# The router of a mixture of experts reads the raw residual instead of the normed one

## The reference

```python
x = x + concatenate([y_d, y_m]) @ w_out
h = rms_norm(x, norm2_g)            # x * rsqrt(mean(x*x) + 1e-6) * norm2_g
g_logits = h @ router_group         # [256, 4], softmax, argmax: the token's group
e_logits = h @ router_expert[g]     # 8 logits of that group, the 2 largest win
# each token goes to 2 of 32 experts; expert: (silu(h @ w_gate) * (h @ w_up)) @ w_down
x = x + weighted sum of the two experts' outputs
```

## Time and profile before

| What | us |
|---|---|
| median of 3 runs | 1144.38 |
| lowest and highest | 1142.68, 1144.67 |
| the profiled execution | 1147.17 |
| its span, first to last instruction | 1145.4 |
| busy in the span: PE, DVE, ACT, POOL | 1077.5, 568.5, 413.7, 48.3 |
| mean granted clock of TensorE | 0.97 of full |

### The profile page before, as it was taken

One profiled execution on the slowest core, in us unless ns is written; L12 is line 12 of the kernel. 1 busy time (PEld: TensorE's weight loads), 2 busy tenths in 40 slices (PEclk: granted clock), 3 DMA queues, 4 the chain that ended last, 5 costly groups with the idle time before them and its releaser, 6 DMA issues.

```text
span 1145.4 us, 13701 instructions
## 1 busy us (share of the span) xinstructions
PE 1077.5 (94%) x5547; PEld 819.3 (72%) x5547; DVE 568.5 (50%) x712; ACT 413.7 (36%) x518; POOL 48.3 (4%) x56
## 2 busy tenths in 40 slices
PE   7996889999999999999999999958899999999996
PEld 6885875544444457888887998837688887888885
DVE  5667552222222236444445448387665654454453
ACT  4446231111111133343343445363344334334332
POOL 2430000000000000000000000010100000000000
PEclk9998999999999999999999999867899999999999
DMA  8961087989999937655655455411075545555540
GB/s 285 300 230 74 15 352 314 366 350 404 415 414 408 421 118 243 188 179 183 187 179 183 135 182 172 150 42 38 1 236 186 184 147 161 188 182 181 186 147 37
DMA packets 101814, 239.51 MB, mean 209 GB/s; under 512 B 11666, under 2 KB 56810, under 8 KB 86282
## 3 DMA queue, kind: packets, MB, share of 16 engines
q1 hardware_dynamic: 99850, 229.05, 55.5%
q0 software_dynamic: 1920, 9.85, 2.5%
HBM read 237.81 MB, written 3.43 MB: 211 GB/s over the span
## 4 chain that ended last, share of the span: by engine, by line
PE 87%; DVE 8%; ACT 3%; issue 1%; POOL 1%; POOLq 0%; DVEq 0%; ACTq 0%
PE banks L924 20%; PE banks L926 19%; PE banks L925 19%; PE banks L1127 10%; PE banks L1142 5%; PE banks L1108 3%; PE banks L1117 3%; PE banks L931 2%; PE banks L1242 1%; PE banks L1056 1%; DVE token_major L1457 1%; PE banks L943 1%; PE banks L1025 1%; PE banks L1009 1%; DVE head_stats L1603 1%
## 5 line engine op out<-in xcount | busy, mean ns | idle before, releaser
L1477 DVE TENSOR_TENSOR weights_lo<-raw_weights,weights_hi 128x2048 fp32r<-128x2048 f32 x116 | 265.7, 2292 | 229.1 <-ACT weights_hi L616 228.9
L616 ACT ACTIVATE weights_hi<-raw_weights 128x2048 fp32r<-128x2048 f32 x116 | 221.6, 1912 | 194.6 <-PE banks L926 184.6
L924 PE MATMUL banks<-weights_hi,normed_T_hi 128*128 128x512 f32 (+1 forms) x624 | 247.2, 396 | 5.0 <-DVE stage L1793 3.1
L926 PE MATMUL banks<-weights_hi,normed_T_lo 128*128 128x512 f32 (+1 forms) x624 | 242.8, 389 | 0.0
L925 PE MATMUL banks<-weights_lo,normed_T_hi 128*128 128x512 f32 (+1 forms) x624 | 242.3, 388 | 0.0
L924 PEld LDWEIGHTS banks<-weights_hi,normed_T_hi 128*128 128x128 f32 x624 | 118.1, 189 | 36.6 <-issue 10.1
L926 PEld LDWEIGHTS banks<-weights_hi,normed_T_lo 128*128 128x128 f32 x624 | 117.8, 189 | 24.8
L925 PEld LDWEIGHTS banks<-weights_lo,normed_T_hi 128*128 128x128 f32 x624 | 117.9, 189 | 22.5
L1127 PE MATMUL banks<-expert_weights,stage 128*64 128x512 f32 x256 | 113.2, 595 | 0.0
L924 PE MATMUL banks<-weights_hi,ffn_hidden_T_hi 128*128 128x512 f32 x176 | 68.6, 390 | 3.0 <-DVE ffn_hidden_T_lo L1797 3.0
L925 PE MATMUL banks<-weights_lo,ffn_hidden_T_hi 128*128 128x512 f32 x176 | 68.5, 389 | 0.0
(11 more groups left out here) (306 smaller groups left out, 1573.6 us busy)
## 6 DMA issues: line engine op xcount, KB each, us to landing
raw_weights<-in_w_in SPq DMA_DIRECT2D x38, 1024.0 KB, 5.2
raw_weights<-in_ffn_w_gate SPq DMA_DIRECT2D x44, 512.0 KB, 3.9
raw_weights<-in_ffn_w_up SPq DMA_DIRECT2D x44, 512.0 KB, 4.9
raw_weights<-in_ffn_w_down SPq DMA_DIRECT2D x22, 1024.0 KB, 4.8
expert_weights<-in_w_gate SPq DMA_DIRECT2D x16, 1024.0 KB, 7.3
expert_weights<-in_w_up SPq DMA_DIRECT2D x16, 1024.0 KB, 9.5
expert_weights<-in_w_down SPq DMA_DIRECT2D x16, 1024.0 KB, 9.6
stage<-in_w_down SPq DMA_DIRECT2D x9, 1024.0 KB, 11.5
```

Of the source, the lines that this page charges most:

```text
L616: ins = eng.activation(w_hi[:, slot, :], raw, ACT.Copy)
L924: eng.matmul(dst, x[0], w[0], start=first_one, stop=False)
L926: return eng.matmul(dst, x[1], w[0], start=False, stop=last_one)
L1477: ins = eng.tensor_tensor(w_lo[:, slot, :], raw, w_hi[:, slot, :], ALU.subtract)
```

## The change

The router reads `res` itself, and what the norm does to it is put elsewhere. The weight of the norm, `norm2_g`, is loaded a second time as one number per feature (`route_gain`) and multiplied into the router's weights on DVE; rstd is applied to the logits when DVE takes them from PSUM. So PE can transpose `res` as soon as it is complete. The ten warming matmuls ahead of the transposes are gone. ACT squares a tile and splits a tile in turn. The normed rows `tok` are now made after the low parts of `routed_T`, and their own low part is made by POOL instead of DVE.

```diff
+        route_gain = sb("route_gain", [P, KT])
 @@ SP, after the pieces 3 to 5
+            eng.dma_start(route_gain[:, :], A["norm2_g"][0].rearrange("(p k) -> p k", k=KT)).then_inc(router_loaded, 16)
 @@ POOL
             eng.wait_ge(normed, TILES * (N2 + 1))
             load_gain("ffn1_norm_2")
+            for t in range(TILES):
+                eng.wait_ge(tok_hi, t + 1)
+                eng.tensor_tensor(tok_parts[1][:, t], tok[:, t, :].rearrange("p (d k) -> p k d", k=KT), tok_parts[0][:, t],
+                                  ALU.subtract).then_inc(tok_lo, 1)
 @@ ACT, c == 3 of the projection loop
-                    eng.wait_ge(router_loaded, 16 * (1 + GROUPS))
+                    eng.wait_ge(router_gained, 1)
 @@ ACT, behind w_out
-            square(N2, lambda t: (gemm_used, 3 + t))
-            t8_split(T_N2, routed_T)
+            square_of(0)
+            raw_split(0)
+            square_of(1)
+            raw_split(1)
             for t in range(TILES):
+                eng.wait_ge(normed, TILES * N2 + t + 1)
                 eng.activation(tok_parts[0][:, t], tok[:, t, :].rearrange("p (d k) -> p k d", k=KT), ACT.Copy).then_inc(tok_hi, 1)
 @@ PE
             eng.wait_ge(gemm_used, 3)
-            stay_warm(10, 0)
-            transpose8(T_N2, tok, lambda t: (normed, TILES * N2 + t + 1), True)
+            transpose8(T_N2, res, lambda t: (gemm_used, 3 + t), True)
             stay_warm(8, 2)
 @@ DVE, projection loop
+                if c == 2:
+                    eng.wait_ge(router_loaded, 16 * (2 + GROUPS))
+                    eng.tensor_tensor(router[:, :, :], router[:, :, :], wide(route_gain[:, :], ROUTES), ALU.mult).then_inc(router_gained, 1)
 @@ DVE, behind w_out
-            norm(N2, lambda t: add_to_residual("w_out", 1, t, 1))
-            t8_split(T_N2, routed_T)
-            for t in range(TILES):
-                eng.wait_ge(tok_hi, t + 1)
-                eng.tensor_tensor(tok_parts[1][:, t], ...)
+            def raw_rest(t):
+                eng.wait_ge(t8_hi, TILES * T_N2 + t + 1)
+                ...
+                eng.tensor_tensor(lo, src, hi, ALU.subtract).then_inc(t8_lo, 1)
+
+            add_to_residual("w_out", 1, 0, 1)
+            add_to_residual("w_out", 1, 1, 1)
+            first_root = mean_root(TILES * N2)
+            raw_rest(0)
+            second_root = mean_root(TILES * N2 + 1)
+            raw_rest(1)
+            for t, taken in enumerate((first_root, second_root)):
+                eng.wait_ge(root_out, taken)
+                eng.wait_ge(gain_loaded, 16 * GB[N2])
+                eng.scalar_tensor_tensor(tok[:, t, :], res[:, t, :], rstd[...], gain[:, :], ALU.mult, ALU.mult).then_inc(normed, 1)
             eng.wait_ge(route, TILES)
-            link(eng.tensor_copy(rt[:, :, 4:40], PS[:, 0:TILES, 0:ROUTES]))
-            link(eng.tensor_tensor(rt[:, :, 4:40], rt[:, :, 4:40], PS[:, 0:TILES, ROUTES:2 * ROUTES], ALU.add))
+            link([eng.tensor_scalar(rt[:, t, 4:40], PS[:, t, 0:ROUTES], rstd[...], None, ALU.mult) for t in each][-1])
+            link([eng.scalar_tensor_tensor(rt[:, t, 4:40], PS[:, t, ROUTES:2 * ROUTES], rstd[...], rt[:, t, 4:40],
+                                           ALU.mult, ALU.add) for t in each][-1])
```

More of the change, by code:

```diff
@@ L257, in two_blocks @@
         gemm_used = sem("gemm_used")
+        raw_ready, router_gained = sem("raw_ready"), sem("router_gained")
         route, route_exp_in, route_exp, assigned = sem("route"), sem("route_exp_in"), sem("route_exp"), sem("assigned")
@@ L706, in _, with square_of, raw_split @@
             feed(13, BEFORE_MOE)
-            square(N2, lambda t: (gemm_used, 3 + t))
-            t8_split(T_N2, routed_T)
+            def square_of(t):
+                eng.wait_ge(gemm_used, 3 + t)
+                eng.activation(tok[:, t, :], res[:, t, :], ACT.Square, accum_out=ss[:, TILES * N2 + t:TILES * N2 + t + 1]).then_inc(squared, 1)
+            def raw_split(t):
+                eng.wait_ge(t8, TILES * T_N2 + t + 1)
+                eng.activation(routed_T[0][:, :, t * P:(t + 1) * P], PS[:, 4 + 2 * t:6 + 2 * t, :].rearrange("p b (k q) -> p (b k) q", q=P),
+                               ACT.Copy).then_inc(t8_hi, 1)
+            square_of(0)
+            raw_split(0)
+            square_of(1)
+            raw_split(1)
             for t in range(TILES):
+                eng.wait_ge(normed, TILES * N2 + t + 1)
                 eng.activation(tok_parts[0][:, t], tok[:, t, :].rearrange("p (d k) -> p k d", k=KT), ACT.Copy).then_inc(tok_hi, 1)
@@ L1643, in _ @@
                 add_to_residual("w_out", 0, t)
-            norm(N2, lambda t: add_to_residual("w_out", 1, t, 1))
-            t8_split(T_N2, routed_T)
-            for t in range(TILES):
-                eng.wait_ge(tok_hi, t + 1)
-                eng.tensor_tensor(tok_parts[1][:, t], tok[:, t, :].rearrange("p (d k) -> p k d", k=KT), tok_parts[0][:, t],
-                                  ALU.subtract).then_inc(tok_lo, 1)
+            def raw_rest(t):
+                eng.wait_ge(t8_hi, TILES * T_N2 + t + 1)
+                src = PS[:, 4 + 2 * t:6 + 2 * t, :].rearrange("p b (k q) -> p (b k) q", q=P)
+                hi, lo = [x[:, :, t * P:(t + 1) * P] for x in routed_T]
+                eng.tensor_tensor(lo, src, hi, ALU.subtract).then_inc(t8_lo, 1)
[8 more added lines that the diff above has]
+                eng.wait_ge(gain_loaded, 16 * GB[N2])
+                eng.scalar_tensor_tensor(tok[:, t, :], res[:, t, :], rstd[:, TILES * N2 + t:TILES * N2 + t + 1], gain[:, :],
+                                         ALU.mult, ALU.mult).then_inc(normed, 1)
             eng.wait_ge(route, TILES)
@@ L1654, in _ @@
             each = range(TILES)
-            link(eng.tensor_copy(rt[:, :, 4:40], PS[:, 0:TILES, 0:ROUTES]))
-            link(eng.tensor_tensor(rt[:, :, 4:40], rt[:, :, 4:40], PS[:, 0:TILES, ROUTES:2 * ROUTES], ALU.add))
+            link([eng.tensor_scalar(rt[:, t, 4:40], PS[:, t, 0:ROUTES], rstd[:, TILES * N2 + t:TILES * N2 + t + 1], None, ALU.mult)
+                  for t in each][-1])
+            link([eng.scalar_tensor_tensor(rt[:, t, 4:40], PS[:, t, ROUTES:2 * ROUTES], rstd[:, TILES * N2 + t:TILES * N2 + t + 1],
+                                           rt[:, t, 4:40], ALU.mult, ALU.add) for t in each][-1])
             link(eng.tensor_copy(rt8[:, :, 0, 0:GROUPS], rt[:, :, 4:4 + GROUPS]))
```

## The result

| | before | changed |
|---|---|---|
| median, 11 runs each | 1144.17 us | 1148.30 us |
| lowest, highest | 1142.23, 1146.84 | 1144.67, 1149.79 |
| ratio, 95% interval | | 1.0033 (1.0021 to 1.0045) |
| profiled execution, its span | 1147.17, 1145.4 | 1147.28, 1145.6 |

The change costs 2.4 to 5.1 us. The two profiled executions hide it: they differ by 0.1 us, because single executions spread by 4.6 us (before) and 5.1 us (changed). So the traces are compared in the stretch that the change touches, counted from the end of w_out, and several traces of each kernel are used.

A forecast was written before the change was run, and what follows sets the result against it. PE was taken as the bound, with changes counting only where it idles or runs slowly between w_out and the experts. Hold +1.7 and clock +0.8 gave +2.5 us, a median of 1146.9 us, range 1140.5 to 1150.5.

The forecast's parts named there:

- Front half: From w_out to the logits: router matmuls start 2.4 us earlier, DVE's routing chain 3.1 us earlier.
- POOL's duration: Each of POOL's two low-part subtractions takes 3.25 us, between 2.35 and 4.6; POOL is done at 167.5.
- The hold: DVE's routing instructions stand still until POOL's subtractions end; +1.7 us taken, +0.9 or +2.2 by where it starts.
- the one from L1657: Hold variant: DVE's routing chain already stands at L1657, if POOL's second instruction gets in first; +2.2 us.
- The clock: PE idles 6.5 us ahead of the position matmuls, so more work runs at 1.2 GHz: 0.8 us, between 0 and 1.3.
- Early part: The small DMA on SP's queue and the weight multiply on DVE cost nothing; without cover 0.5 to 1 us.
- No hold: Rival: POOL and DVE run side by side, the gather comes 2.8 us earlier; 1140.5 to 1141.6 us; chance 0.15.
- POOL fast with only two-input instructions held: Rival: POOL's subtractions take 2.35 to 2.8 us, one-input DVE instructions run on; 1144.0 us, no change; chance 0.17.
- POOL fully slowed (4.6): Rival: POOL's strided subtractions take about 4.6 us each, +4.3 and 1 for the clock; 1149.7 us; chance 0.13.
- Weights set the pace: Rival: loading the experts' weights bounds the expert loop, so the shift doesn't reach the end; 1144.4 us; chance 0.05.

The follow-up runs named there:

- x5: The kernel before plus the early part alone (DMA of norm2_g, multiply on DVE, ACT's wait): 1144.60 us, ratio 1.0000.
- x6: The changed kernel without its early part (no DMA of norm2_g, no multiply by it): 1151.08 us, ratio 1.0058.
- x2: The changed kernel with the low parts of the token rows back on DVE, none on POOL: 1147.57 us, ratio 1.0030.
- x11: The changed kernel run once more, unchanged, for a second trace: 1148.95 us, ratio 1.0034 against the kernel before.
- x1: The changed kernel with 14 instead of 8 warming matmuls behind the transposes: 1149.97 us, ratio 1.0043.
- x3: The changed kernel with the edits of x1 and x2 together: 1148.92 us, ratio 1.0029.
- x7: x3 with DVE writing the normed rows in the order of the parts, and 22 instead of 12 warming matmuls ahead of the positions: 1144.13 us, ratio 0.9993.
- x9: x3 with 26 instead of 12 warming matmuls ahead of the positions: 1145.99 us, ratio 1.0016.
- x10: x1 with 29 instead of 12 warming matmuls ahead of the positions: 1146.20 us, ratio 1.0017.
- x4: The kernel before with one part of the change alone, POOL making the low parts of the token rows: 1146.42 us, ratio 1.0015.

## Why the prediction was right

Where the time went: w_out to first expert is 26.99, 25.53 and 25.50 us with the router of before, mean 26.0, and 28.30, 29.81 and 29.72 with the changed one, mean 29.3: +3.3 us, within the measured 2.4 to 5.1. Up to the positions it is +1.34 in every trace (16.8 and 18.16); from there on +1.9 in the mean (9.2 and 11.1), and single traces give 0 to 3. With three traces on each side, one of each being x5 or x6, the 1.9 is the less certain of the two.

- **Front half.** Right: router at 5.36 us after w_out, forecast 5.5. What I missed is the gap of 1.47 us ahead of it, though my own numbers held it (transposes until 154.5, then eight warming matmuls, router at 157.8). In the traces of the changed kernel and of x6 the half clock starts during the router matmuls, in x2, with the same gap, at their end; in the first they took 6.2 us, not 3.75. That made the logits there no earlier than before (11.8 against 11.7); in x11 they came at 10.3. With that gap covered (x1, x3, x7, x9, x10) the front's half clock is 0 or 3.4 us long and not 3.4 to 10.2, so it gets shorter and isn't always gone. It cost nothing at the positions only because DVE was held anyway (x1).
- **POOL's duration.** 2.84 us against 3.25 forecast and a lower end of 2.35: the step costs POOL 0.5 us, half of ACT's and DVE's excess. POOL ended 14.55 after w_out, forecast 15.2.
- **The hold.** Right, and shown by x1, x2, x4 and x10, with 4.52 us as the longest. Of the three variants the one from L1657 applied (here L1691): the first copy was caught. The forecast for it was +2.2; POOL ended 0.6 us earlier, and the copy ended with POOL and did not start behind it, which makes +1.3. That this is close to the +1.7 that I took is partly luck: I had put the hold on a later instruction, which is too small, and made POOL too slow, which is too large. The Trainium skill, "SBUF — State Buffer", section "Who interferes with whom", says that a copy can enter a two-port mode and then wait for a GpSimd instruction that came first; the traces agree (0.17 us grows to 1.85, 2.13, 4.05 and 4.52, and the copy from PSUM stays at 0.23).
- **The clock.** Right in sign, too small: 0.8 forecast, 1.9 in the mean. The gap ahead of the positions was not 6.5 us but 1.39 in the first trace, since the router matmuls and the warming themselves ran at half clock, and 3.02 in the second. x2 and x3 show that the clock costs without the hold too: with none they stay 3 us above before, and only 0.5 of it is there at the positions. x9 and x10 show that covering the gap ahead of the positions takes away the 6.8 us on positions and gather, one trace each. Why the half clock at the front comes and goes between executions of the same instructions stays open.
- **Early part.** Nothing, as forecast, within 1.1 us (x5). Its multiply takes 0.45 us on DVE in the changed kernel's trace.
- **Rivals.** No hold: falls to x1. POOL fast with only two-input instructions held: its duration was nearly right, but the one-input copy was held too. POOL fully slowed (4.6): falls to the 2.84. Weights set the pace: falls, since the loop takes 243.3 to 243.6 us in every trace wherever it starts.
- The point forecast, +2.5 us, is below the middle of what was measured by 1.3 us; the term that was mis-sized is the clock (0.8 against 1.9), while the hold was 0.4 too large.

Left open: why x6's set lies 2.8 us above the changed kernel's, and what decides in a single execution where the half clock falls.

## What to carry to other kernels

Before a piece of work goes to POOL, look at what DVE does at that moment: here DVE's copy within SBUF stood still until both of POOL's back-to-back instructions were through, and two-input instructions on SBUF did so until the one that ran was the earlier trace rows, so a chain of small instructions is the worst neighbour and a wait of DVE the best place. A step that is made shorter ahead of a bound that stays (here the low parts, on POOL or on DVE) only turns into an idle PE, and in these traces an idle of 3 us and more came with half clock each time; shorten the bound first, as x7 does, or keep the warming. A stretch at half clock that starts while two kernels still run the same instructions is no effect of the edit: look where it starts before crediting it. Where single executions spread as widely as the effect, compare traces by landmarks counted from a common event, and take several.

## What the runs showed of the hardware that was not expected

- A waiting DVE instruction was not let in between two POOL instructions without a pause between them, whose semaphore was already up (x1: 4.05 us, into both; x6, x10 and x11 alike). In the earlier trace rows POOL waits for the end of its own first instruction and pauses by some 0.08 us, and DVE gets in. That the pause makes the difference is likely and not tested.
- The same program has its half-clock time in different places from run to run: 0.88 and 0.77 mean clock in the attention stage (86 to 130 us) of the kernel before. Its w_out ended 3.0 us later in the second trace, where the clock from 130 to 150 us was 0.91 and not 1.00 as well.
- A scaling of 128x1024 elements on DVE takes 1.94 us when it writes at a step of 128 elements and reads contiguously, against 1.24 with both contiguous (x7; the changed kernel's two scalings take 2.47 together). A step cost DVE about the same in a write as in a read: its subtraction takes 2.05 us with one input at a step of eight and 1.25 with both contiguous (x7).
